# Forgetting attention on one core: where the inverse row sums are turned and spread, and how two key tiles' transposes and products follow each other

## The chip, the cores and the metric

One core of one Trainium2 chip runs one launch of a two-block transformer layer. The metric is device time in microseconds (us) of that launch, lower is better. The matmul engine is TensorE (PE, with its weight loads as PEld), VectorE is DVE, ScalarE is ACT, GpSimd is POOL, and SyncE (SP) issues the DMAs.

## The reference, cut to what matters

The launch runs a first block (retention, sliding-window attention, an MLP), then a second (pooling mixer, forgetting attention, an MLP), all in fp32 on 1024 tokens of width 1024. The change touches only the forgetting attention of the second block: 8 heads of 64, 1024 queries, causal, with a bias from summed log forget gates.

```python
log_f = jax.nn.log_sigmoid(f_logit.astype(jnp.float32)).transpose(0, 2, 1)
cf = jnp.cumsum(log_f, axis=-1)
...
    s = jnp.einsum('bhqd,bhkd->bhqk', qb, k, preferred_element_type=jnp.float32) * scale
    s = s + cq[..., :, None] - cf[..., None, :]
    s = jnp.where(kpos[None, :] <= qpos[:, None], s, NEG_INF)
    p = jax.nn.softmax(s, axis=-1)
    return jnp.einsum('bhqk,bhkd->bhqd', p.astype(v.dtype), v)
```

## The kernel before, in words

Every product is made in fp32r from a high part and a low part of each operand, so most come as two or three matmuls. Large weight products fill the span before and after the attention; the attention runs from about 1695 to 1843 us.

**Units and steps.** The work is cut into 16 units u: 4 pairs of heads t, for each the lower and the upper half of the queries (Q = 0, 1), for each both heads j of the pair. `ITEMS` lists the 8 items idx = (t, Q), so u = 2 idx + j. A unit has four query tiles ii. Its scores have 128 to 512 keys for Q = 0 and 640 to 1024 for Q = 1. `attention_order` (L373) is the one order that all engines follow: at step s and tile ii it does the scores of the next tile, the exponentials of tile (s, ii), and then, for unit s-1, one "turn" (Q = 0) or two (Q = 1). A turn n is one tile of 128 keys.

- `scores` (L1021): TensorE makes query x key products (L1049, L1050) and adds the mask (L1051). VectorE takes the row minimum of the negated scores (L2397). The two score bank pairs alternate, so a tile's scores wait for the exponential of the tile two before it.
- `weights` (L1662): ScalarE takes the exponential into `Pu`, and the row sum into `st` (L1667).
- `turned` (L1056): TensorE transposes up to four 128x128 tiles of `Pu` into one PSUM bank (L1062), ScalarE copies it as the high part `PAh` (L1675), VectorE subtracts to get the low part `PAl` (L2402).
- `values` (L1067) of turn n - `LAG` (2): value x `PAh` and value x `PAl` (L1078, L1079) add up the unit's output in bank 6 or 7.

The transposed tiles take turns in two PSUM banks, 4 and 5 (`ring.turn([4, 5])`, L1007). A turn therefore waits for `PAl` of the turn two before it. The same ring also serves the two small products below, each of which takes one place in it and shifts the banks of the turns behind.

**The end of a unit (`tail`).** After the last `values` of a unit a generator is advanced once per turn. VectorE computes the inverse sums of both heads of an item (`inverse`, L2408: four small instructions, L2415, L2418, L2422, L2423) when the first head's unit ends; ScalarE copies half of the output bank to `ot` (L1687), VectorE adds (L2435). Two advances later TensorE transposes the inverse sums `n4` to rows (bank group `nT`, L1095) for j = 0, and ScalarE copies them to `rw` (L1693); for j = 1 TensorE spreads them over 128 partitions with one product (`rl`, L1103), and VectorE multiplies the output by that bank (L2440). POOL then splits the scaled output into the high and low parts (L2659, L2661) that the output projection reads. POOL also prepares the next pair's operands (`stack`, L2606), and SyncE copies them by DMA (L2983, L2985).

Where each small piece stands before, in the order of a turn:

```python
for _ in range(1 + ITEMS[(s - 1) // 2][1] if s else 0):
    turned(n, *TURNS[n])
    if n >= LAG:
        values(n - LAG, *TURNS[n - LAG])
        ...
    for g in tails:
        next(g, None)
```

## Time and profile before

| what | value |
|---|---|
| median of 3 runs | 2570.13 us (2567.49 to 2576.94) |
| profiled execution | 2573.41 us, its span 2571.6 us |
| mean granted TensorE clock | 0.998 of full |
| DVE, ACT, POOL busy, whole span | 57%, 41%, 7% |
| share of PE in the chain that ended last | 89% |
| attention (first scores to the last spreading product) | about 1695.5 to 1842.6 us |
| first scores of the third pair of heads | 1762.0 us |

The profile counts an engine as busy while an instruction is in flight. TensorE's matmuls overlap: a row of the timeline tells when each started, and the distance between two starts is what one costs in a full pipe. In a timeline row the columns are start, duration, engine, line, operation, output<-inputs, shape and count, and in brackets the idle time before it with what ended it.

### The profile page before, as it was taken

What the parts mean: (1) busy time and instruction counts of PE and PEld (TensorE: products, weight loads), DVE (VectorE), ACT (ScalarE), POOL (GpSimd) and SP (SyncE); (2) the same over time, 40 slices, a digit from 0 to 9 for tenths busy, and PEclk for the clock granted to TensorE, in tenths of its full rate; (3) what the DMA queues carried; (4) which work ended last, traced back from release to release, by engine and by line L of the source; (5) the groups of instructions that cost most, each with busy time, mean ns of one, the idle gap of its engine ahead of it and who ended that gap; (6) DMA issues with size and microseconds to landing.
All of it is one profiled execution on the core that took longest, in us unless ns stands there. A gap on an engine that the chain in (4) does not pass through costs nothing.

```text
span 2571.6 us, 30682 instructions
## 1 busy us (share of the span) xinstructions
PE 2524.5 (98%) x12072; PEld 2084.9 (81%) x12072; DVE 1473.5 (57%) x2153; ACT 1056.3 (41%) x1698; POOL 189.0 (7%) x173
## 2 busy tenths in 40 slices
PE   7999999999999999999999999999999999999998
PEld 6777888888888788888888887877788888888886
DVE  4345223323533777666664754358768676576668
ACT  4344322223212544444434543357526444444432
POOL 0000000000020200000000110154111000000000
PEclk9999999999999999999999999999999999999999
DMA  4221211111422426547865541111313464588554
GB/s 165 67 73 66 74 41 42 34 33 66 147 82 82 143 87 218 184 150 260 306 249 183 185 157 59 34 26 34 115 50 131 140 225 137 175 319 327 183 191 166
DMA packets 129679, 347.59 MB, mean 135 GB/s; under 512 B 13152, under 2 KB 13408, under 8 KB 129408
## 3 DMA queue, kind: packets, MB, share of 16 engines
q1 hardware_dynamic: 129536, 345.63, 38.5%
q8 instruction: 96, 1.57, 0.3%
q14 instruction: 47, 0.39, 0.0%
HBM read 256.91 MB, written 85.52 MB: 133 GB/s over the span
## 4 chain that ended last, share of the span: by engine, by line
PE 89%; DVE 5%; issue 3%; DMA 1%; ACT 1%; POOL 1%; SPq 0%; DVEq 0%; ACTq 0%; POOLq 0%
PE bank L635 27%; PE bank L637 27%; PE bank L636 27%; DVE PAl L2402 1%; DVE st L2397 1%; PE bank L696 1%; POOL accX L2584 1%; PE bank L1062 1%; PE bank L746 1%; PE bank L813 1%; DMA rbx<-wp_d 0%; PE bank L817 0%; PE bank L823 0%; PE bank L781 0%; DVE wlo L1735 0%
## 5 line engine op out<-in xcount | busy, mean ns | idle before, releaser
L1735 DVE TENSOR_TENSOR wlo<-raw,whi 128x1024 fp32r<-128x1024 f32 x102 | 125.2, 1235 | 254.1 <-ACT whi L1138 253.4
L635 PE MATMUL bank<-hhi,whi 128*128 128x512 f32 x608 | 249.6, 411 | 1.7 <-DVE hlo L1760 1.7
L637 PE MATMUL bank<-hhi,wlo 128*128 128x512 f32 x608 | 239.3, 394 | 0.0
L636 PE MATMUL bank<-hlo,whi 128*128 128x512 f32 x608 | 238.6, 392 | 0.0
L1138 ACT ACTIVATE whi<-raw 128x1024 fp32r<-128x1024 f32 x102 | 106.6, 1054 | 103.9 <-PE bank L637 88.2
L635 PEld LDWEIGHTS bank<-hhi,whi 128*128 128x128 f32 x608 | 115.1, 189 | 29.0 <-issue 6.7
L637 PEld LDWEIGHTS bank<-hhi,wlo 128*128 128x128 f32 x608 | 114.9, 189 | 25.2
L636 PEld LDWEIGHTS bank<-hlo,whi 128*128 128x128 f32 x608 | 115.3, 190 | 22.3
L1443 ACT ACTIVATE r<-r 128x512 f32<-128x512 f32 x78 | 49.1, 629 | 137.6 <-DVE r L2220 100.0
L635 PE MATMUL bank<-yhi,whi 128*128 128x512 f32 x192 | 75.0, 391 | 0.0
L637 PE MATMUL bank<-yhi,wlo 128*128 128x512 f32 x192 | 74.8, 390 | 0.0
L636 PE MATMUL bank<-ylo,whi 128*128 128x512 f32 x192 | 74.8, 390 | 0.0
L635 PE MATMUL bank<-whi,hhi 128*128 128x256 f32 x256 | 74.4, 290 | 0.0
L636 PE MATMUL bank<-wlo,hhi 128*128 128x256 f32 x256 | 72.5, 283 | 0.0
L637 PE MATMUL bank<-whi,hlo 128*128 128x256 f32 x256 | 72.5, 283 | 0.0
L635 PE MATMUL bank<-uw0bh,uw0ah 128*128 128x512 f32 x176 | 68.9, 391 | 0.8 <-DVE uw0bl L2172 0.7
L636 PE MATMUL bank<-uw0bl,uw0ah 128*128 128x512 f32 x176 | 68.6, 390 | 0.0
L637 PE MATMUL bank<-uw1bh,uw1al 128*128 128x512 f32 x176 | 68.6, 390 | 0.0
L637 PE MATMUL bank<-uw0bh,uw0al 128*128 128x512 f32 x176 | 68.6, 390 | 0.0
L635 PE MATMUL bank<-uw1bh,uw1ah 128*128 128x512 f32 x176 | 68.6, 390 | 0.0
L636 PE MATMUL bank<-uw1bl,uw1ah 128*128 128x512 f32 x176 | 68.6, 390 | 0.0
L2593 POOL TENSOR_TENSOR accX<-accX,acc 128x1024 f32<-128x1024 f32 x8 | 20.2, 2519 | 609.7 <-DVE acc L2279 609.7
(477 smaller groups left out, 7206.6 us busy)
## 6 DMA issues: line engine op xcount, KB each, us to landing
ra<-ud_d SPq DMA_DIRECT2D x112, 512.0 KB, 4.5
raw<-wp_d SPq DMA_DIRECT2D x102, 512.0 KB, 3.5
rbh<-wp_d SPq DMA_DIRECT2D x64, 512.0 KB, 5.7
rawp<-wp_d SPq DMA_DIRECT2D x26, 1024.0 KB, 5.8
ud_d<-us SPq DMA_DIRECT2D x104, 256.0 KB, 5.4
rbw<-wp_d SPq DMA_DIRECT2D x48, 512.0 KB, 3.6
ud_d<-f SPq DMA_DIRECT2D x76, 256.0 KB, 2.0
rbx<-wp_d SPq DMA_DIRECT2D x32, 512.0 KB, 7.6
```

Of the source, the lines that this page charges most:

```text
L635: e.matmul(P, sh, mh, start=first, stop=False, skip_group_check=more)
L636: e.matmul(P, sh, ml, start=False, stop=False, skip_group_check=more)
L637: return e.matmul(P, sl, mh, start=False, stop=last, skip_group_check=more)
L696: i = e.transpose(P[:, 128 * j:128 * j + 128], src[:, 128 * k:128 * k + 128], ident[:, :])
L746: i = e.matmul(P[:, 256 * (m % 2) + j0:256 * (m % 2) + 256], qs[64 * g:64 * g + 64, m, 128 * n:128 * n + 128], ks[64 * g:64 * g + 64, 128 ...
L813: x = e.matmul(P[:, 0:256], ss[n % 2][:, :], rv[i][:, n, :], start=True, stop=n == 0)
L1062: x = e.transpose(P[:, 128 * ii:128 * ii + 128], Pu[u % 2][ii][:, 128 * k:128 * k + 128], ident[:, :])
L1138: e.activation(whi[n % SLOTS][:, :], raw[n % RAWS][:, :], ACT.Copy).then_inc(*up("whi", n))
L1443: e.activation(r[:, :], r[:, :], ACT.Relu).then_inc(*up("relu", tag, name, p))
L1735: e.tensor_tensor(out=wlo[n % SLOTS][:, :], in0=raw[n % RAWS][:, :], in1=whi[n % SLOTS][:, :].bitcast(F32), op=ALU.subtract).then_inc(*up( ...
L2397: e.tensor_reduce(st[:, m:m + 1], psum[:, b:b + w], AXIS.X, ALU.min).then_inc(*up("mn", u, ii))
L2402: e.tensor_tensor(out=PAl[n % 3][:, c], in0=bank_of("pt", n)[:, c], in1=PAh[n % 3][:, c].bitcast(F32), op=ALU.subtract).then_inc(*free("pt ...
```

## The change

In `attention_order` two callbacks take the place of the later part of the tails. `rows` (transpose of the inverse sums on TensorE, copy to `rw` on ScalarE) is called at tile ii = 2 of every even step from 2, right after the scores and exponentials and ahead of the turns. `spread` (the spreading product, the multiplication on VectorE, the split on POOL) is called at ii = 3 of every odd step from 3, also ahead of the turns, and once at the end. And where a step has two turns per tile, both turns' transposes are issued first, then both turns' products. The number and size of the instructions stay the same.

```diff
@@ -370,7 +370,8 @@
     return max(0, k - 4 * ITEMS[u // 2][1])
 
 
-def attention_order(scores, weights, stack, turned, values, tail, pooled):
+def attention_order(scores, weights, stack, turned, values, tail, rows, spread, pooled):
+
 
     restack, tails = iter(()), []
     scores(0, 0)
@@ -383,23 +384,30 @@
                 scores(*divmod(4 * s + ii + 1, 4))
             if s < 16:
                 weights(s, ii)
+            if ii == 2 and s > 1 and s % 2 == 0:
+                rows(s // 2 - 1)
+            if ii == 3 and s > 2 and s % 2:
+                spread((s - 3) // 2)
             next(restack, None)
             if s == 0:
                 pooled(ii)
-            for _ in range(1 + ITEMS[(s - 1) // 2][1] if s else 0):
+            group = range(n, n + 1 + ITEMS[(s - 1) // 2][1]) if s else ()
+            for n in group:
                 turned(n, *TURNS[n])
+            for n in group:
                 if n >= LAG:
                     values(n - LAG, *TURNS[n - LAG])
                     if TURNS[n - LAG][0] < TURNS[n - LAG + 1][0]:
                         tails.append(tail(TURNS[n - LAG][0]))
                 for g in tails:
                     next(g, None)
-                n += 1
+            n += 1 if s else 0
     for m in range(n - LAG, n):
         values(m, *TURNS[m])
     tails.append(tail(15))
     for g in tails:
         run(g)
+    spread(7)
 def build(nc, I, out, sg, cd, yd, xd, ud):
     with ExitStack() as ctx:
         return programs(nc, ctx, I, out, sg, cd, yd, xd, ud)
@@ -1083,26 +1091,23 @@
             else:
                 x.then_inc(*up("val", n))
 
-        def tail(u):
-            idx, j, t, Q = unit_of(u)
-            yield
-            yield
-            if j == 0:
-                P, free = ring.open("nT", idx)
-                e.wait_ge(*free)
-                e.wait_ge(*ok("n4", idx))
-                for ii in range(4):
-                    x = e.transpose(P[0:34, 128 * ii:128 * ii + 128], n4[:, 34 * ii:34 * ii + 34], ident[:, :])
-                x.then_inc(*ring.full("nT", idx))
-            else:
-                P, free = ring.open("rl", idx)
-                e.wait_ge(*free)
-                e.wait_ge(*ok("free", "nT", idx))
-                if idx == 0:
-                    e.wait_ge(*ok("n40", 2))
-                e.matmul(P[:, :], sel[:, :], rw[:, :], start=True, stop=True).then_inc(*ring.full("rl", idx))
-
-        attention_order(scores, nothing, lambda t: idle(8), turned, values, tail, pooled)
+        def rows(idx):
+            P, free = ring.open("nT", idx)
+            e.wait_ge(*free)
+            e.wait_ge(*ok("n4", idx))
+            for ii in range(4):
+                x = e.transpose(P[0:34, 128 * ii:128 * ii + 128], n4[:, 34 * ii:34 * ii + 34], ident[:, :])
+            x.then_inc(*ring.full("nT", idx))
+
+        def spread(idx):
+            P, free = ring.open("rl", idx)
+            e.wait_ge(*free)
+            e.wait_ge(*ok("free", "nT", idx))
+            if idx == 0:
+                e.wait_ge(*ok("n40", 2))
+            e.matmul(P[:, :], sel[:, :], rw[:, :], start=True, stop=True).then_inc(*ring.full("rl", idx))
+
+        attention_order(scores, nothing, lambda t: idle(8), turned, values, lambda u: idle(2), rows, spread, pooled)
         tally.alias(("att_end",), ring.latest)
         ring.turn(range(8))
 
@@ -1685,14 +1690,14 @@
             if u > 1:
                 e.wait_ge(*ok("free", "ov", u - 2))
             e.activation(ot[own, :], bank_of("ov", u)[o:o + 64, :], ACT.Copy).then_inc(*up("oal", u))
-            yield
-            if j == 0:
-                e.wait_ge(*ok("full", "nT", idx))
-                if idx:
-                    e.wait_ge(*ok("full", "rl", idx - 1))
-                e.activation(rw[:, :], bank_of("nT", idx)[0:34, :], ACT.Copy).then_inc(*free("nT", idx))
-
-        attention_order(nothing, weights, lambda t: idle(8), turned, nothing, tail, pooled)
+
+        def rows(idx):
+            e.wait_ge(*ok("full", "nT", idx))
+            if idx:
+                e.wait_ge(*ok("full", "rl", idx - 1))
+            e.activation(rw[:, :], bank_of("nT", idx)[0:34, :], ACT.Copy).then_inc(*free("nT", idx))
+
+        attention_order(nothing, weights, lambda t: idle(8), turned, nothing, tail, rows, nothing, pooled)
         feed.cap = NPIECES
         e.wait_ge(*ok("clo", 7))
         feed.ahead(CAT + 5)
@@ -2433,13 +2438,14 @@
             if j == 0 and idx > 1:
                 e.wait_ge(*ok("clo", idx - 2))
             e.tensor_tensor(out=o[own, :], in0=bank_of("ov", u)[own, :], in1=ot[own, :], op=ALU.add).then_inc(*free("ov", u))
-            yield
-            if j:
-                e.wait_ge(*ok("free", "ov", u))
-                e.wait_ge(*ok("full", "rl", idx))
-                e.tensor_tensor(out=o[:, :], in0=o[:, :], in1=bank_of("rl", idx)[:, :], op=ALU.mult).then_inc(*free("rl", idx))
-
-        attention_order(scores, nothing, lambda t: idle(8), turned, nothing, tail, pooled)
+
+        def spread(idx):
+            o = ov[idx % 2]
+            e.wait_ge(*ok("free", "ov", 2 * idx + 1))
+            e.wait_ge(*ok("full", "rl", idx))
+            e.tensor_tensor(out=o[:, :], in0=o[:, :], in1=bank_of("rl", idx)[:, :], op=ALU.mult).then_inc(*free("rl", idx))
+
+        attention_order(scores, nothing, lambda t: idle(8), turned, nothing, tail, nothing, spread, pooled)
         feed.cap = NPIECES
         feed.ahead(CAT + 5)
 
@@ -2648,12 +2654,9 @@
         run(stack(0))
         ones_rows()
 
-        def tail(u):
-            idx, j, t, Q = unit_of(u)
-            if j == 0:
-                return
+        def spread(idx):
+            t, Q = ITEMS[idx]
             c = slice(512 * Q, 512 * Q + 512)
-            yield from idle(4)
             e.wait_ge(*ok(*latest))
             e.wait_ge(*ok("free", "rl", idx))
             e.tensor_copy(chi[4 + t][:, c], ov[idx % 2][:, :]).then_inc(*up("cho", idx))
@@ -2662,7 +2665,7 @@
                             op=ALU.subtract).then_inc(*up("clo", idx))
             latest[:] = "clo", idx
 
-        attention_order(nothing, nothing, stack, nothing, nothing, tail, nothing)
+        attention_order(nothing, nothing, stack, nothing, nothing, lambda u: idle(2), nothing, spread, nothing)
         e.wait_ge(*ok("wt_end", 2))
         e.wait_ge(*ok(*latest))
         e.tensor_copy(chi4[:, :], chi[4][:, :].bitcast(F32)).then_inc(*up("chi4", 0))
```

## Rows read from the trace of the kernel before

**Rows 1.** The page, busy time of TensorE over the whole span.
```profile
PE 2524.5 (98%) x12072; PEld 2084.9 (81%) x12072; DVE 1473.5 (57%) x2153; ACT 1056.3 (41%) x1698; POOL 189.0 (7%) x173
```
**Rows 2.** Windows: stretch, length, busy of PE, PEld, DVE, ACT, POOL, granted clock, DMA.
```profile
1702.00:1842.00 140.00, 127.77 (x769) 96.71 (x767) 119.94 (x217) 108.92 (x247) 58.91 (x63) 0.98 0.13 31
1717.00:1753.00 36.00, 32.84 (x202) 25.09 (x202) 32.03 (x57) 29.08 (x67) 22.58 (x24) 0.99 0.17 39
```
**Rows 3.** Waits, 1695 to 1850 us: us in total, times, longest.
```profile
DVE PAl L2402 <- ACT PAh L1675: 14.4, 23, 1.4
...
PE bank L1095 <- DVE PAl L2402: 6.6, 7, 1.3
```
**Rows 4.** Timeline of TensorE, the first transpose of inverse sums, item 0.
```profile
1713.66 0.23 PE L1051 MATMUL bank<-maskb,identb 128*128 128x128 bf16 x1
...
1715.71 0.34 PE L1079 MATMUL bank<-PAl,v 128*128 128x384 f32 x1
1717.05 0.61 PE L1095 MATMUL bank<-ident,n 128*34 128x128 f32 x4 [1.00 <-DVE PAl L2402]
1717.96 0.51 PE L1049 MATMUL bank<-KH,QS 128*128 128x512 f32 x1 [0.29 <-ACT Pu L1667]
```
**Rows 5.** Timeline of VectorE, the same place.
```profile
1714.95 0.58 DVE L2423 TENSOR_TENSOR n<-st,nh 128x8 f32<-128x8 f32 x1
1715.46 1.21 DVE L2397 TENSOR_REDUCE st<-bank 128x1 f32<-128x1024 f32 x1
...
1719.04 0.96 DVE L2397 TENSOR_REDUCE st<-bank 128x1 f32<-128x768 f32 x1 [0.52 <-PE bank L1051]
```
**Rows 6.** Timeline of ScalarE, the same place.
```profile
1714.46 0.37 ACT L1675 ACTIVATE PAh<-bank 128x256 fp32r<-128x256 f32 x1
1714.86 0.59 ACT L1687 ACTIVATE ot<-bank 64x512 f32<-64x512 f32 x1
1716.70 1.11 ACT L1667 ACTIVATE Pu<-bank,st 128x1024 f32<-128x1024 f32 x1 [1.24 <-DVE st L2397]
...
1717.96 0.58 ACT L1693 ACTIVATE rw<-bank 34x512 fp32r<-34x512 f32 x1
```
**Rows 7.** Timeline of TensorE, the other transposes of inverse sums with a long wait.
```profile
1733.23 0.61 PE L1095 MATMUL bank<-ident,n 128*34 128x128 f32 x4 [0.67 <-DVE PAl L2402]
...
1750.90 0.61 PE L1095 MATMUL bank<-ident,n 128*34 128x128 f32 x4 [1.28 <-DVE PAl L2402]
...
1786.60 0.61 PE L1095 MATMUL bank<-ident,n 128*34 128x128 f32 x4 [1.31 <-DVE PAl L2402]
...
1835.58 0.62 PE L1095 MATMUL bank<-ident,n 128*34 128x128 f32 x4 [1.33 <-DVE PAl L2402]
```
**Rows 8.** Timeline of VectorE, the multiplication by the spread sums.
```profile
1724.44 0.68 DVE L2440 TENSOR_TENSOR ov<-ov,bank 128x512 f32<-128x512 f32 x1
```
**Rows 9.** Timeline of TensorE: product pair and next transposes, at two clocks.
```profile
1721.42 0.47 PE L1078 MATMUL bank<-PAh,v 128*128 128x512 f32 x1
...
1721.97 0.60 PE L1062 MATMUL bank<-ident,Pu 128*128 128x128 f32 x4
...
1838.47 0.77 PE L1078 MATMUL bank<-PAh,vrest 128*128 128x512 f32 x1
...
1839.47 0.63 PE L1062 MATMUL bank<-ident,Pu 128*128 128x128 f32 x2
```
**Rows 10.** Timeline of POOL, the last operand of the third pair's preparation.
```profile
1749.43 1.26 POOL L2630 TENSOR_TENSOR QS<-q,QS 64x512 fp32r<-64x512 f32 x1
```
**Rows 11.** Windows around the two drops of the granted clock, and an earlier one.
```profile
1750.00:1754.00 4.00, 2.64 (x11) 1.87 (x12) 4.00 (x7) 2.51 (x5) 0.69 (x1) 0.76 0.17 37
1835.00:1839.00 4.00, 2.85 (x14) 2.19 (x15) 2.40 (x4) 1.34 (x3) 0.00 (x0) 0.80 0.41 135
...
1512.00:1515.00 3.00, 3.00 (x23) 2.74 (x22) 2.90 (x2) 2.21 (x5) 2.05 (x1) 1.00 0.02 5
```
**Rows 12.** Chain of waits, sixteen transposes of another stage in a row.
```profile
1512.34 1.75 PE bank L696 x16
```

## The prediction

> **What bounds the kernel now.** I read the page first: TensorE is in flight 98% of the span [rows 1], so the time moves only where TensorE's stream gets shorter or loses an idle stretch. The windows come next, cut to the one stage that the diff touches. In the attention from 1702 to 1842 us VectorE is busy 119.9 of 140 us, ScalarE 108.9, TensorE in flight 127.8; from 1717 to 1753 VectorE has 32.0 of 36 [rows 2]. No engine is full: three take turns in being late, VectorE most. The reader is to see that this caps the change: all of VectorE's idle time there is 140 - 119.9 = 20.1 us, 0.8% of the kernel, and a reordering can win only part of it. The waits then say what is late: VectorE waits 14.4 us for the copies PAh, and TensorE 6.6 us in seven places ahead of the transposes of the inverse sums, each time for the PAl that frees the bank [rows 3]. Five of the seven are shown: 1.00, 0.67, 1.28, 1.31 and 1.33 us [rows 4, 7]. These waits are what the moved pieces stand in.
>
> **The change, part by part.** It adds and removes no instruction, so each cost is one of position. Items alternate between one turn per tile (Q = 0) and two (Q = 1), and the cases differ.
>
> *1. Transposing the inverse sums, items with Q = 0 (four).* Today it stands behind the turn of ii = 3 and waits for a PAl [rows 4]. Now it stands ahead of the turn of ii = 2, one turn earlier, when VectorE has not finished the inverse: its last instruction ends at 1714.95 + 0.58 = 1715.53 [rows 5]. TensorE would be there after the mask product of 1713.66, which costs under 0.1: it stands 1.8 us, longer than today's 1.00. Behind it is the turn's own transposes, and behind those, on ScalarE, a whole row: the sums' transposes end 0.61 later at 1716.14, the copy to rw takes 0.58 (to 1716.7), the turn's PAh 0.4 (1717.1), the copy to ot 0.59 (1717.7), and only then the exponential of 1024 keys, which started at 1716.70 today [rows 6]. It is 1.0 late. The scores at 1717.96 wait for just that exponential [rows 4], and VectorE's next minimum, at 1719.04, for those scores [rows 5]. So I put +1.0 on three of the four places. The fourth, at 1750.90, is followed by a half-clock stretch [rows 11] in which VectorE waits for other reasons: 0. Sum +3.0. The bounds of one place: -1.0 if the removed wait is all won, +1.8 if TensorE's stand is all lost.
>
> *2. The same, items with Q = 1 (three; the fourth has no scores left behind it and stays as it is, 1.33 us and all [rows 7]).* The inverse comes two tiles earlier here, so it is ready. The transposes move behind one tile's scores, and the bank's PAl is done by then. That removes 6.6 - 1.00 - 1.28 - 1.31 - 1.33 = 1.7 us of waits in three places. Given back: the second turn's transposes need the bank that the copy to rw frees. The small transposes take about 0.44 (their 0.61 overlaps the next), the copy 0.58 behind their end, so that turn starts some 0.4 later than in a full pipe. Taken: -0.5 in each, -1.5 in sum, because VectorE, which sets the pace, saves the idle and pays only part of the 0.4. Bounds per place -0.9 and +0.4.
>
> *3. Spreading the sums.* The product moves from behind a turn to behind a tile's scores. Where one turn follows (three items) its bank is needed a tile later: 0. Where two follow (four items), the second one needs the bank that VectorE's multiplication frees. The multiplication (0.68 us [rows 8]) stands behind a minimum and now ahead of the two PAl. Its cover is that the first turn's PAh takes 0.6 anyway; about 0.3 of it shows. Sum +1.2; bounds 0 and 0.7 each. For POOL the split now stands ahead of steps of the operand preparation and waits for that multiplication. The cover: the third pair's preparation ends at 1750.7 [rows 10], 11 us ahead of its first use at 1762.0; cost 0, and even if it stood 2 us longer it would be 0. SP's copies of those operands move with it, under the same cover.
>
> *4. Two turns' transposes in a row.* Today a product pair of 0.55 us (1721.42 to 1721.97 [rows 9]) lies between the two turns' transposes. Without it the second turn is ready 0.55 earlier, of which ScalarE, busy 0.6 with the first copy, can use some 0.3. Against it: the first pair of products now stands behind the second turn's wait. In the Q = 1 scores (four steps) VectorE has no idle time to fill. What remains is one tile in each of three steps where two turns meet small scores: -0.9. Bounds: 0, and 24 tiles x 0.27 = -6.5.
>
> Sum: 3.0 - 1.5 + 1.2 - 0.9 = **+1.8 us**. The profiled execution took 2573.4, so it would take 2575.2; it stood 3.3 above the median, within the runs' own spread. On the median that is 2570.1 + 1.8 = **2571.9**. A measurement of this kernel can tell about 0.5%, 12.9 us, from no change.
>
> **Rivals.**
>
> *The waits are really won (faster).* If VectorE catches up from item 1's lateness in its 20 us of idle time, part 1 is 0 or below: its four removed waits (1.00, 1.28, 1.31 and a small one) become a gain of about 3, with parts 2 and 4 about -5.5. For it: this wait is TensorE's longest in the stage [rows 3]. Against it: ScalarE's order is fixed, and it holds the exponential back [rows 6]. Time: 2564.6.
>
> *The clock falls more often (slower).* Granted clock fell to 1.2 GHz, half, twice in the attention: the windows from 1750 and from 1835 show 0.76 and 0.80, and ahead of each TensorE had stood 1.3 us for the inverse sums [rows 7, 11]. After the equally long stand at 1786.60 and the 1.00 at 1717.05 it did not. At half clock a product pair to the next transposes takes 1839.47 - 1838.47 = 1.00 instead of 0.55 [rows 9], and three such pairs cost 1.4 us. With stands of 1.8 in place of 1.3 it might fall in all four places of part 1: three more drops, +4.2, on top of the 1.8: 2576.1. It decides from the point where a stand is followed by a drop in more than one of the four.
> *The clock falls under rows of transposes (slower).* Part 4 puts up to eight transposes side by side. If that by itself brought a drop in each of the eight units with two turns, at 1.4 us each, the time would be 2571.9 + 11.2 = 2583.1. Against it: sixteen transposes in a row, 1.75 us long, ran with the granted clock at 1.00 [rows 11, 12]. I give it 3%. The Trainium skill ("TensorE: Matmul & The Clock Gate", Part 4: PE-mode transpose) speaks for it: a transpose "doesn't count as PE-busy the same way". The trace does not agree as far as those sixteen go; by the page the 2583.1 would be the likelier time, by the trace the 2571.9.
>
> *The change does nothing.* If the order of the small pieces is absorbed wholly by VectorE's load, all four parts are 0: 2570.1. Also, the sums' product would then not stand "behind" a finished inverse at all where Q = 0, which is what part 1 says.
>
> **How the numbers follow.** Forecast (+0.5 to +4 us) 45%; waits won 27%; nothing 12%; clock by stands 10%; clock by transposes 3%; something else 3%. The likeliest gives 2571.9. For the range I take in the won waits (2564.6) and the clock rival (2576.1), and the runs' spread of some 2 us around a median of three, cut where 2 in 10 are left out: 2564.5 to 2577.5. Only a case that goes past 12.9 us leaves the middle: the gain would have to be two thirds of VectorE's idle time, 2%; the loss would need all upper bounds at once (4 x 1.8 + 3 x 0.4 + 4 x 0.7 = 11.2) with clock drops, or the drops under transposes, 4%.
>
> **What would show each step right or wrong.** Part 1: in the timeline of the changed kernel the first sums' transposes start at the end of L2423 and not of a PAl, with about 1.8 us idle before, and the exponential behind them begins about 1 us later relative to its minimum. Part 2: near 1733 they start with no wait, and the second turn's transposes wait for ScalarE's rw. Part 3: the transposes behind a spreading product wait for L2440. Part 4: VectorE's wait for PAh (14.4 us) shrinks by under 2 us. Clock: the windows tell how many stretches are at half clock. The length from the first scores to the last spreading product, 147 us now, should be about 149. I am wrong if it is under 145 or over 153.

## The result, and the profile after

The changed kernel takes 2581.76 us (median of 7 runs, 2578.14 to 2582.34) where the kernel before, beside it, takes 2570.13 (7 runs, 2567.06 to 2576.94): a ratio of 1.0043, 95% interval 1.0034 to 1.0052. It is slower by 0.43%. That lies inside the 0.5% that I had called no change, but 4.3 us above the upper end of my range, and my forecast of +1.8 us was wrong: it is +11.6. The profiled execution took 2582.21 us, its span is 2580.4.

All of it is in the attention. Measured from the start of the first scores to the start of the last spreading product, the attention took 146.6 us before (1695.51 to 1842.12) and 157.85 after (1693.80 to 1851.65), +11.25. By the sign given beforehand ("wrong if under 145 or over 153") the working is wrong, not only its size.

The page and the windows of the changed kernel (stretch, length, busy of PE, PEld, DVE, ACT, POOL, granted clock, DMA), which answer to [rows 1, 2, 11]. Its lines are those of before plus 4 to 8: transposes L1070, products L1086 and L1087, scores L1057 to L1059, copy PAh L1680, PAl L2407, sums' transposes L1099, spreading product L1108.

```profile
PE 2524.2 (98%) x12072; PEld 2084.5 (81%) x12072; DVE 1475.4 (57%) x2153; ACT 1057.0 (41%) x1698; POOL 189.8 (7%) x173
```
```profile
1701.00:1851.00 150.00, 127.86 (x764) 98.50 (x763) 120.97 (x216) 109.25 (x246) 59.44 (x62) 0.98 0.12 29
...
1750.00:1754.00 4.00, 2.45 (x16) 1.95 (x16) 2.94 (x4) 3.11 (x5) 3.71 (x5) 1.00 0.30 70
1801.00:1805.00 4.00, 3.56 (x16) 3.25 (x16) 1.58 (x4) 1.37 (x5) 1.89 (x2) 0.61 0.00 0
1839.00:1843.00 4.00, 4.00 (x20) 3.73 (x18) 1.23 (x4) 1.72 (x4) 1.56 (x2) 0.57 0.00 0
```

The busy times are the same as before, over 150 us instead of 140: each engine does the same work and waits longer. There are two stretches at half clock, as before, in other places, so the clock does not fall more often; what the two cost is worked out under *Two parts at a time*. The mean granted clock of the 7 runs is 0.9966, that of 31 runs of before 0.9965. The waits are (who waits <- whose work ended it: us in total, times, longest), 1693 to 1853 us, against [rows 3]:

```profile
DVE PAl L2407 <- ACT PAh L1680: 21.3, 41, 1.4
ACT PAh L1680 <- PE bank L1087: 15.3, 22, 1.2
ACT PAh L1680 <- PE bank L1070: 10.2, 20, 1.4
...
PE bank L1057 <- ACT Pu L1672: 5.4, 6, 1.9
PE bank L1099 <- DVE n L2428: 5.4, 4, 1.7
PE bank L1108 <- DVE PAl L2407: 3.4, 4, 1.0
```

Four things are to be seen. VectorE's wait for PAh grew from 14.4 to 21.3 us, where I had it shrink. TensorE's wait ahead of the sums' transposes did not go away, it changed its cause: 5.4 us for the inverse (L2428), plus 1.1 in one place for a PAl, where 6.6 stood. The spreading product (L1108) waits for a PAl in four places, 3.4 us, where the kernel before has four waits of 0.1. And the second row is of a kind that the kernel before does not have at all: ScalarE's copy PAh is held back 22 times, 15.3 us in all, by a *product* (L1087). I had named neither of these two.

The three signs of parts 1 to 3 are all there. Timeline of TensorE of the changed kernel, first item, then at 1725 and at 1733 us (start, duration, line, output<-inputs, shape, and in brackets the idle time with what ended it), against [rows 4, 7]:

```profile
1711.98 0.23 PE L1059 MATMUL bank<-maskb,identb 128*128 128x128 bf16 x1
1713.93 0.60 PE L1099 MATMUL bank<-ident,n 128*34 128x128 f32 x4 [1.72 <-DVE n L2428]
...
1717.33 0.50 PE L1057 MATMUL bank<-KH,QS 128*128 128x512 f32 x1 [0.94 <-ACT Pu L1672]
...
1727.60 0.33 PE L1070 MATMUL bank<-ident,Pu 128*128 128x128 f32 x1 [0.45 <-DVE ov L2446]
...
1733.62 0.61 PE L1099 MATMUL bank<-ident,n 128*34 128x128 f32 x4
1734.25 0.66 PE L1070 MATMUL bank<-ident,Pu 128*128 128x128 f32 x4
1735.32 0.55 PE L1070 MATMUL bank<-ident,Pu 128*128 128x128 f32 x3 [0.41 <-ACT rw L1698]
```

The stand of 1.72 us until the inverse is done (I said 1.8; in the other three places of part 1 it is 1.48, 1.47 and 0.72); at 1727.60 the wait for VectorE's multiplication behind a spreading product; at 1733.62 no wait, and then 0.41 for the copy to rw (I said 0.4). VectorE and ScalarE at the first item, against [rows 5, 6]:

```profile
1713.71 1.21 DVE L2402 TENSOR_REDUCE st<-bank 128x1 f32<-128x1024 f32 x1
```
```profile
1714.57 0.59 ACT L1698 ACTIVATE rw<-bank 34x512 fp32r<-34x512 f32 x1 [1.71 <-PE bank L1099]
1715.06 0.36 ACT L1680 ACTIVATE PAh<-bank 128x256 fp32r<-128x256 f32 x1
1715.45 0.59 ACT L1692 ACTIVATE ot<-bank 64x512 f32<-64x512 f32 x1
1716.07 1.11 ACT L1672 ACTIVATE Pu<-bank,st 128x1024 f32<-128x1024 f32 x1
```

The minimum ended at 1713.71 + 1.21 = 1714.92, the exponential started at 1716.07: 1.15 us later, where before it was 0.03. That is part 1 as predicted, at this place. What was left to explain was therefore mainly part 4.

### The profile page after: what moved, and what is told of

Same layout as the page of the kernel before. It is cut to its first block, busy times and chain, and to the rows that moved or that the text cites. A ratio compares the mean times of both kernels' runs of the same rounds, so it can differ in the third digit from the quotient of the medians.

```text
span 2580.4 us, 30682 instructions
## 1 busy us (share of the span) xinstructions
PE 2524.2 (98%) x12072; PEld 2084.5 (81%) x12072; DVE 1475.4 (57%) x2153; ACT 1057.0 (41%) x1698; POOL 189.8 (7%) x173
## 4 chain that ended last, share of the span: by engine, by line
PE 90%; DVE 4%; issue 2%; ACT 2%; DMA 1%; POOL 1%; SPq 0%; DVEq 0%; ACTq 0%; POOLq 0%
PE bank L643 28%; PE bank L645 28%; PE bank L644 28%; PE bank L1070 1%; DVE PAl L2407 1%; PE bank L704 1%; POOL accX L2590 1%; PE bank L754 1%; PE bank L821 1%; DVE st L2402 1%; ACT PAh L1680 0%; PE bank L831 0%; PE bank L825 0%; PE bank L789 0%; DVE wlo L1740 0%
## 5 line engine op out<-in xcount | busy, mean ns | idle before, releaser
L2407 DVE TENSOR_TENSOR PAl<-bank,PAh 128x512 fp32r<-128x512 f32 (+1 forms) x96 | 52.6, 555 | 22.5 <-ACT PAh L1680 21.3
```

Of the source, the lines that this page charges most:

```text
L2407: e.tensor_tensor(out=PAl[n % 3][:, c], in0=bank_of("pt", n)[:, c], in1=PAh[n % 3][:, c].bitcast(F32), op=ALU.subtract).then_inc(*free("pt ...
```

## The experiments

All kernels but the fourth-buffer ones differ from before or after in order and in banks alone; every one computes the whole layer. "Step s" is the stretch from the first scores of unit s to those of unit s+1 (step 15: to the last spreading product), from the timeline of TensorE. The parts became switches:

```diff
+            if ii == 2 and s > 1 and s % 2 == 0 and s // 2 - 1 in ROWS_MOVED:
+                rows(s // 2 - 1)
+            if ii == 3 and s > 2 and s % 2 and (s - 3) // 2 in SPREAD_MOVED:
+                spread((s - 3) // 2)
...
+            group = list(range(n, n + 1 + ITEMS[(s - 1) // 2][1])) if s else []
+            for part in ([group] if PAIRED else [[m] for m in group]):
+                for n in part:
+                    turned(n, *TURNS[n])
+                for n in part:
+                    if n >= LAG:
+                        values(n - LAG, *TURNS[n - LAG])
```

An item that is not moved has its piece in the tail, as before. All results, the kernel before being run beside each group (medians 2569.7 to 2570.8). The ratio is that of the record and not the quotient of two medians (for e1 the medians give 1.0013). The attention is that of one profiled execution each:

| run | pairs | rows moved | spread moved | banks, buffers | median us | ratio, 95% | attention us | half-clock stretches |
|---|---|---|---|---|---|---|---|---|
| before | | | | | 2570.1 | | 146.60 | 2 |
| after | x | x | x | | 2581.76 | 1.0043, 1.0034 to 1.0052 | 157.85 | 2 |
| e1 | x | | | | 2574.02 | 1.0004, 0.9994 to 1.0013 | 150.03 | 0 |
| e2 | | x | | | 2574.41 | 1.0013, 1.0003 to 1.0022 | 150.44 | 1 |
| e3 | | | x | | 2569.13 | 0.9994, 0.9984 to 1.0004 | 144.94 | 0 |
| e4 | | x | x | | 2574.51 | 1.0012, 1.0002 to 1.0021 | 151.06 | 1 |
| e5 | x | x | x | own banks | 2574.64 | 1.0014, 1.0005 to 1.0024 | 150.97 | 1 |
| e6 | | | x | own banks | 2565.24 | 0.9976, 0.9967 to 0.9985 | 141.99 | 1 |
| e7 | | Q = 1 items | | | 2570.86 | 1.0005, 0.9995 to 1.0014 | 144.51 | 0 |
| e8 | | x, one tile later | x | own banks | 2564.60 | 0.9976, 0.9966 to 0.9985 | 140.10 | 0 |
| e9 | x | x, one tile later | x | own banks | 2569.25 | 0.9990, 0.9980 to 1.0000 | 144.69 | 0 |
| e10 | x | | x | | 2576.36 | 1.0025, 1.0015 to 1.0034 | 151.93 | 2 |
| e11 | x | x | | | 2580.59 | 1.0040, 1.0026 to 1.0054 | 155.43 | 2 |
| e12 | | x, one tile later | two-turn places and the end | own banks | 2563.71 | 0.9973, 0.9964 to 0.9983 | 140.09 | 0 |
| e13 | x | | | nT own, third bank | 2569.74 | 0.9996, 0.9987 to 1.0005 | 144.92 | 0 |
| e14 | | | | nT own, third bank | 2565.63 | 0.9984, 0.9975 to 0.9993 | 139.91 | 0 |
| e15 | | as e12 | as e12 | e12 + third bank | 2563.40 | 0.9971, 0.9960 to 0.9981 | 139.03 | 0 |
| e16 | x | | | nT own | 2572.49 | 1.0007, 0.9997 to 1.0016 | 149.31 | 1 |
| e17 | x | | | 4th PAh, PAl | 2572.31 | 1.0003, 0.9994 to 1.0013 | 147.34 | 0 |
| e18 | x | | | e13 + 4th PAh, PAl | 2567.24 | 0.9983, 0.9974 to 0.9992 | 143.59 | 1 |

Where a half-clock stretch falls varies, so steps are compared where neither kernel has one.

**The parts alone, and all but the pairs.**

```diff
+ROWS_MOVED = ()            # range(8) in e2, e4
+SPREAD_MOVED = ()          # range(8) in e3, e4
+PAIRED = True              # e1; False in e2, e3, e4
```

> Two turns' transposes first, then two turns' products; the two small products where they were before. Time against before, and length of the attention (146.6 us before, 157.9 after the whole change). Ring theory (a small product ahead of a pair of turns takes one of only two PSUM banks): no small product is moved, so -1 to +1 us, attention about 147. Inverse theory (the transposes of the inverse sums wait for an unfinished inverse): 0 as well. Pairs theory (products now stand behind the second turn's wait): +5 us or more, attention above 151.

> Only the transposes of the inverse sums are moved, in all eight items. Inverse theory: TensorE's stands of 1.0 to 1.9 us in four places cost all they last, +7 us or more, attention above 153. Ring theory: +1 to +4 us, since the stands are partly won back by the wait that is gone, and only the items with two turns pay for the bank. Pairs theory: 0.

> Only the spreading product (with its multiplication and split) is moved. Ring theory: about +1 to +1.8 us in each of the four places ahead of a pair of turns, so +4 to +7 us, attention 151 to 154. Inverse theory and pairs theory: 0, attention 146 to 148.

> The whole change but for the pairs: both small products moved, turns one by one as before. Ring theory: most of the 11 us stays, +7 to +10. Inverse theory: all of it stays, +10 to +12. Pairs theory: most of it goes, +4 or less.

These texts set three theories against each other. The ring theory failed in e3 (attention 144.94, where it had 151 to 154), the inverse theory in e4 (151.06, 4.5 us above before, where it had 10 to 12); the pairs theory came near in e1 (150.03, where it had above 151) and in e4 (it had +4 or less), and e2 (+3.8) lies in the range of the ring theory.

No single part makes the 11 us. The ratios of e1, e2 and e3 add up to 1.0011, the whole is 1.0043; e4 without pairs is 1.0012, so the pairs cost 0.3% on top of the rest. Steps without a half-clock stretch say where (us):

| step | before | e1 pairs | e2 rows | e3 spread | e4 rows, spread | after |
|---|---|---|---|---|---|---|
| 2 + 3 | 17.92 | 18.47 | 18.98 | 17.08 | 18.21 | 18.31 |
| 4 | 9.79 | 10.73 | 9.81 | 11.01 | 11.03 | 11.55 |
| 5 | 5.02 | 5.42 | 5.02 | 5.03 | 5.03 | 5.42 |
| 6 | 7.08 | 7.08 | 9.45 | 7.39 | 9.28 | 9.29 |

Rows moved: +1.06 in steps 2 + 3. Pairs: +0.55 there, then +0.94 and +0.40, in each of the steps 3 to 5 where I had put nothing or a gain. The waits of e1, 1694 to 1846 us:

```profile
DVE PAl L2426 <- ACT PAh L1699: 14.6, 29, 1.1
ACT PAh L1699 <- PE bank L1106: 11.8, 23, 0.9
```

L1106 is the product on PAl. So the new wait comes with the pairs alone.

**A kernel before without its drops.** e7 moves the rows of items 1, 3, 5, 7 only:

```diff
+ROWS_MOVED = (1, 3, 5, 7)
```

> The transposes of the inverse sums are moved only in the items with two turns per tile, where the inverse is long done. Inverse theory: moving them in all items cost 3.8 us of attention, all of it in the items with one turn, so here -1 to +0.5 us against before. Ring theory: +1 to +2 us, since the second turn waits for the copy that frees the bank.

Its steps are those of before within 0.04 us, but for the two in which before has a half-clock stretch (step 7: 13.77 against 12.89; step 15: 24.69 against 23.46). So this part of the change is worth nothing, and e7's trace, all at full clock, is the base for what follows: 144.51 us. The two stretches cost before 0.9 + 1.2 us.

**Order or bank?** A transpose group, `nT` and `rl` all take places in the ring of two PSUM banks. e5 is the whole change with the spreading products of even items in bank 1 and the sums' transposes of odd items in bank 3, both of the score banks that are free there; e6 does it with the spread moved only; e8 calls `rows` of the Q = 0 items one tile later (ii = 3); e9 is e8 with pairs; e12 is e8 with the spread moved only where two turns follow (items 0, 2, 4 and 6), and at the end.

The waits of the scores that make these banks free in time are not shown.

```diff
-            P, free = ring.open("nT", idx)
+            own_bank = 3 if idx % 2 else None
+            P, free = ring.open("nT", idx, bank=own_bank)
...
-            P, free = ring.open("rl", idx)
+            own_bank = 1 if idx % 2 == 0 else None
+            P, free = ring.open("rl", idx, bank=own_bank)
```
```diff
-            if ii == 2 and s > 1 and s % 2 == 0 and s // 2 - 1 in ROWS_MOVED:
+            if ii == (3 if s % 4 == 2 else 2) and s > 1 and s % 2 == 0 and s // 2 - 1 in ROWS_MOVED:
...
-PAIRED = False
+PAIRED = True
...
-SPREAD_MOVED = range(8)
+SPREAD_MOVED = (0, 2, 4, 6, 7)
```

> The whole change, but the spreading product of four items and the transposes of the inverse sums of the four items with two turns each use a PSUM bank that the scores leave free (1 and 3), so that they take no place between the two banks of the turns. Ring theory (the place in the ring is what a moved small product costs ahead of a pair of turns): the steps with two turns and small scores fall from 11.6 us to 10 or less, three to four of them, so the attention falls from 157.9 to 149 to 153. Pairs theory (a product now stands behind the second turn's wait, whoever holds the bank): it falls by 3 us at most, since pairs alone cost 3.4 us with no small product moved. Inverse theory: no change, 156 to 158.

> Only the spreading product is moved, turns one by one, and the same two own banks. Ring theory: the steps with two turns and small scores fall from 11.0 us (spreading product moved, in the ring) to about 9.0, so the attention is 138 to 141 us and the time 4 to 7 us below before. Theory that those steps are bound by VectorE or by latency in any case: 143 to 145, as with the ring.

> Both small products moved, turns one by one, own banks, and where an item has one turn per tile the transposes of the inverse sums come one tile later (behind the scores of tile 3 instead of 2), when the inverse is finished. Inverse theory: the step before (8.3 us with the transposes at tile 2, 6.2 before) returns to 6.2 to 6.8 and the step behind does not get longer than 11, so the attention is at least 3 us shorter than with the own banks alone, and 138 to 142. If the stand for the inverse is only moved, not removed, it stays at 145 or more.

> The version with both small products moved, own banks and the later transposes of the inverse sums (attention 140.1 us), now with two turns' transposes first and then two turns' products. Only the pairs differ. Pairs theory (a product that was ready waits behind the second turn's bank): +3 to +5 us of attention, 143 to 145.5. Theory that pairs cost only together with a small product in the ring: 139.5 to 141.

> The 140.1 us version, but the spreading product moved only where two turns follow and a bank of its own is free. The step of one turn per tile with large scores was 7.4 us with it moved there and 7.1 before, three of them: so 139 to 139.6 us. If the multiplication has to stand somewhere on VectorE in any case, it stays at 140.1 or goes up.

The banks matter much: e5 takes the whole change from 1.0043 to 1.0014, with step 4 down from 11.55 to 10.33. With own banks the kernel with the spread moved is faster than before (e6, 0.9976, clear of 1; an own bank for the spreading product without the move was not tried). Its attention, 141.99, is just above the 138 to 141 of the ring theory; e5, e8 and e9 lie where the theories named for them had put them. Calling the rows one tile later removes the cost of part 1: steps 2 and 3 of e8 are 6.18 and 10.93 us, in e3, with the rows in the tail, 6.16 and 10.92. It gains nothing either: e8 has the ratio of e6, 0.9976. With pairs, e9 is at 144.69 us, 4.6 above e8. So the pairs cost about as much on a good version as on before. e12 against e8 is nothing: 0.9973 against 0.9976, 140.09 against 140.10 us, where 139 to 139.6 was forecast.

**Two parts at a time.**

```diff
+ROWS_MOVED = ()            # e10; range(8) in e11
+SPREAD_MOVED = range(8)    # e10; () in e11
+PAIRED = True
```

> Pairs and the moved spreading product in the ring, transposes of the inverse sums where they were. The parts alone gave attentions of 150.0 (pairs) and 144.9 (spread), against 144.5 with neither and with the clock never halved. If the parts only add up: 150 to 151. If pairs and a small product in the ring make each other worse: 153 or more, with the step of two turns and small scores at 12 us or more, against 10.7 with pairs alone and 11.0 with the spread alone.

> Pairs and the moved transposes of the inverse sums in the ring, spreading product where it was. The parts alone: 150.0 (pairs) and about 148.5 (transposes, less one halved stretch), 144.5 with neither. If they add up: 153 to 155. If most of what is missing in the whole change (157.9) is between these two: 156 or more. If it is between pairs and spread: 150 to 153.

Neither fits one of its forecasts: e10 (151.93) lies between adding up and making each other worse, e11 (155.43) a little above adding up. By the ratios the pairs go badly with both (e10 1.0025 against 0.9998 for the two alone, e11 1.0040 against 1.0017). By the lengths against the full-clock base of 144.51 there is little left of that: pairs +5.5, rows +5.9 with a half-clock stretch in it, spread +0.4, in sum 11.8 with one stretch; the whole is +13.3 with two. The steps tell more. Adding the parts up step by step (e7 and what e1, e2 and e3 each differ from it), the whole is 2.0 us *below* the sum over the thirteen steps in which none of the five traces has a half-clock stretch. It is above the sum by more than 0.1 us only where it has a stretch itself: step 12 takes 13.14 against 10.14, step 15 25.62 against 24.10. So at full clock the parts do not make each other worse, and by this estimate the two stretches cost the changed kernel some 4.5 us, where the two of before cost 2.1: about 2 of the 11 us are clock. What makes a stretch dearer in one place than in another no run shows.

**Which resource do the pairs run out of?** Two were left: the bank (two turns' transposes in a row need both, so the next pair waits for both PAl), and the buffers PAh, PAl, of which there are three. e13 gives the turns of units 3, 7, 11 and 15 a third PSUM bank and keeps `nT` of odd items out of the ring, with pairs; e14 is the same without pairs; e16 has pairs and `nT` out, no third bank; e15 is e12 with the third bank.

```diff
-            P, free = ring.open("pt", n)
+            third = ITEMS[u // 2][1] and u % 2
+            if k == 0:
+                cycle[:] = [ring.order[ring.at], ring.order[1 - ring.at], 1]
+            P, free = ring.open("pt", n, bank=cycle[k % 3] if third else None)
```

> Pairs alone, with the transposes of the inverse sums of two-turn items in a bank of their own, and in the four units where the scores beside the turns leave bank 1 free the turns go round three banks instead of two. Bank theory of the pairs (the second turn waits for a bank, and ready products stand behind it): in these units the wait between the two turns' transposes goes, and the step of two turns and small scores falls from 10.7 us to 9.3 or less, with the step behind it from 5.4 to 5.0. Theory that rows of transposes cost by themselves: it stays within 0.3 us of the kernel with pairs and two banks.

> The same banks, turns one by one and all small products where they were. If the two banks bind there too: step of two turns and small scores 9.8 us before, 9.0 or less here, last stretch 23.5 before, 22.5 or less. If VectorE or the latency of transposes, copy and subtraction bind: within 0.3 us of 9.8 less the 0.8 us of the removed wait.

> Pairs alone with the transposes of the inverse sums of two-turn items in a bank of their own, two banks for the turns. It tells the third bank from the own bank. Bank theory: the step of two turns and small scores keeps 9.9 to 10.3 us of the 10.7, as the waits between the two turns' transposes are still there. If the small product in the ring was all that pairs cost: 9.3 or less.

> The best version so far (spreading product moved in five items, transposes of the inverse sums later, own banks; attention 140.1 us) with the third bank for the turns. Bank theory: 137 to 139 us. Theory that VectorE binds it by now (126 us busy of 142): 139.5 to 140.5.

Both bank edits together are worth 4.6 us without pairs (e14, 139.91 against 144.51), the third bank by itself about 3 with them (e13 against e16, 149.31 less some 1.5 for e16's half-clock stretch in step 7, 14.95 against 13.46). The pairs go on costing 5.0 us (e13 against e14). So the bank is a limit of this kernel, but not what the pairs suffer from. The waits of ScalarE in e13, then in e14 (the product on PAl is L1115, the transposes L1098):

```profile
ACT PAh L1711 <- PE bank L1115: 9.0, 22, 0.8
ACT PAh L1711 <- PE bank L1098: 4.4, 13, 0.8
```
```profile
ACT PAh L1711 <- PE bank L1098: 10.5, 26, 0.9
```

The wait for the product is there with three banks, and only with pairs. Of the forecasts, e13 missed (step 4 at 9.74 us, where the bank theory had 9.3 or less), e14 (step 4 at 8.64, step 15 at 22.02) and e16 (step 4 at 9.96) came as the bank theory had them, and e15 at 139.03 is at the upper edge of its 137 to 139. ScalarE's copy of turn n writes the buffer of turn n-3 and waits for that turn's product (`val n-3`). e17 adds a fourth PAh and PAl to e1, in memory that is free only from the turns of unit 9 on; e18 does the same to e13.

```diff
+    PAh.append(at("PAh3", FO + 32, [128, 512], F32R))
+    PAl.append(at("PAl3", FO + 34, [128, 512], F32R))
...
-            if n >= 3:
-                e.wait_ge(*ok("val", n - 3))
+            if n == FOURTH:
+                e.wait_ge(*ok("val", 47))
+            elif n >= 3:
+                e.wait_ge(*ok("val", n - (4 if n > FOURTH else 3)))
```

> Pairs alone, but from unit 9 on (step 10 and later, where the values of the second pair of heads are dead and give the room) PAh and PAl have four buffers instead of three, so that ScalarE's copy of turn n waits for the product of turn n-4 and not n-3. Buffer theory of the pairs: in these steps the copy of the second turn no longer waits for a product that stands behind that turn's own transposes; pairs cost 2.2 us there over turns one by one (steps 9 to 15), and at least 1.3 of it goes: last stretch 24.3 to 23.6 or less, step 11 12.55 to 12.1 or less. Bank theory, or TensorE's order alone: nothing changes by more than 0.3 us, though the wait's row gets shorter.

> Pairs with three banks in the steps that have a bank free (144.9 us of attention) and the four buffers from unit 9 on. If buffers and banks are all that pairs cost: steps 12 and 15 fall to those of the three banks with turns one by one, 8.4 and 22.0 (22.7 with pairs). If a part lies in TensorE's order itself, step 15 stays above 22.5.

Because the buffer comes halfway, each of these kernels holds its own control. Windows (columns as above), steps 3 to 8 and steps 11 to 15, of e7 (no pairs, three buffers), e1 (pairs, three) and e17 (pairs, four in the second stretch only):

```profile
1712.21:1768.59 56.38, 50.48 (x316) 38.95 (x317) 49.62 (x90) 44.47 (x100) 34.86 (x39) 1.00 0.17 39
1780.67:1837.61 56.94, 50.74 (x316) 38.38 (x315) 47.75 (x89) 43.59 (x96) 7.97 (x9) 1.00 0.08 24
```
```profile
1713.34:1773.06 59.72, 51.70 (x315) 38.78 (x316) 52.36 (x90) 44.37 (x100) 35.86 (x39) 1.00 0.16 37
1785.54:1844.24 58.70, 52.78 (x315) 38.54 (x314) 48.34 (x89) 43.86 (x96) 7.98 (x9) 1.00 0.08 23
```
```profile
1712.28:1772.04 59.76, 51.71 (x315) 38.79 (x316) 52.38 (x90) 44.38 (x100) 35.88 (x39) 1.00 0.16 37
1784.53:1840.51 55.98, 51.73 (x315) 38.46 (x315) 47.27 (x89) 43.07 (x96) 8.00 (x9) 1.00 0.08 24
```

In the first stretch the pairs cost 3.3 us, with or without the edit (59.72 and 59.76 against 56.38). In the second they cost 1.8 with three buffers (58.70 against 56.94) and nothing with four: 55.98 is 1.0 *below* the unpaired kernel. The wait goes with it; from 1780 us on ScalarE's waits for PAh in e1, then in e17 (product L1106 and L1116, transposes L1089 and L1099):

```profile
ACT PAh L1699 <- PE bank L1106: 6.0, 11, 0.9
...
ACT PAh L1699 <- PE bank L1089: 2.9, 9, 0.8
```
```profile
ACT PAh L1711 <- PE bank L1099: 7.0, 14, 1.0
```

e18 agrees (step 15: 21.28 us, 22.74 in e13, 22.02 in e14), and is faster than before, 0.9983. The forecasts of the buffer theory held in both (e17: step 15 at 22.40, step 11 at 12.04; e18: step 12 at 8.43). The whole runs follow: the fastest of e17 is 2.5 us below the fastest of e1 (2570.19, 2572.68), that of e18 3.6 below that of e13 (2564.45, 2568.02), though the ratios of e17 and e1 (1.0003, 1.0004) do not tell them apart. The fourth buffer was tried with pairs only, so how much of the last 1.0 us belongs to the pairs and how much to the buffer is open, as is the first half, where there was no room for one.

One place shows the mechanism. ScalarE of e1, and TensorE of e1, where unit 11's turns go in pairs:

```profile
1803.01 0.60 ACT L1699 ACTIVATE PAh<-bank 128x512 fp32r<-128x512 f32 x1 [0.28 <-PE bank L1089]
1804.27 0.60 ACT L1699 ACTIVATE PAh<-bank 128x512 fp32r<-128x512 f32 x1 [0.66 <-PE bank L1106]
```
```profile
1802.32 1.39 PE L1089 MATMUL bank<-ident,Pu 128*128 128x128 f32 x8
1803.47 0.47 PE L1105 MATMUL bank<-PAh,vrest 128*128 128x512 f32 x1
1803.78 0.39 PE L1106 MATMUL bank<-PAl,vrest 128*128 128x512 f32 x1
```

Both turns' transposes end at 1802.32 + 1.39 = 1803.71, and ScalarE has been free since 1803.61. But the second copy starts at 1804.27, 0.1 after the end of the *first* product pair behind those transposes (1803.78 + 0.39 = 1804.17). That is 0.56 us lost, about the 0.55 of a product pair, and e1 has 23 such waits.

## Why the prediction was wrong

Against e7 the parts measured, with what I had in brackets: part 1 +5.9 (+3.0), part 2, which is e7 against before, 0 (-1.5), part 3 +0.4 (+1.2), part 4 +5.5 (-0.9).

**Part 4 is the step that failed, in its sign.** I wrote that "without it the second turn is ready 0.55 earlier, of which ScalarE ... can use some 0.3", sum -0.9, and bounded the cost by 0. Measured, it is +5.5 us alone (e1 against e7), +4.6 (e9, e8), +5.0 (e13, e14), in traces with no half-clock stretch in the attention. The fastest whole runs of the same three couples differ by 5.3, 4.0 and 4.9 us, their medians by 3.2, 4.7 and 4.1; the ratios of e1 and e7 alone (1.0004, 1.0005) show no difference, and why is open. The trace of e7 is a good execution of it: granted clock 0.999, where its ten runs have 0.9967 in the mean. I looked at when the second turn's transposes are done, and not at what else its copy needs. In the order of before, products n-2 stand ahead of the transposes of turn n+1, so the copy of turn n+1, which overwrites the buffer of turn n-2, finds it free. In pairs the products n-2 stand behind those transposes, which first wait for a bank. The second turn of each pair can gain nothing from being transposed early, and loses whatever its transposes waited, and at the place shown above, where the timeline has no wait ahead of them, the length of the products themselves. I even wrote that "the first pair of products now stands behind the second turn's wait", and did not ask who waits for that product. VectorE and ScalarE sit in the chain bank, PAh, PAl, bank, so the delay is paid.

**Part 1 was right in three places and wrong in the fourth.** e2 against e7 gives +1.06, +1.09 and +1.11 (steps 2 + 3, 10 + 11, 14 + 15), by the stand and the late exponential as worked out, where I had +1.0. The fourth place I let be 0 because a half-clock stretch follows it in before, and it cost 2.7 us in e2 (steps 6 + 7: 22.64 against 19.97), which has a stretch of its own there. That is not all clock. Between the changed kernel and e10, which differ by the moved rows alone and have both no stretch there, the place costs 1.55 (20.65 against 19.10), where steps 2 + 3 and 10 + 11 cost 1.09 and 1.10. Between the copy to rw and the exponential ScalarE has one copy more there, of a piece of weights, and TensorE stands twice as long for the exponential as at 1717.33:

```profile
1751.60 1.05 ACT L1143 ACTIVATE whi<-raw 128x1024 fp32r<-128x1024 f32 x1
```
```profile
1754.55 0.50 PE L1057 MATMUL bank<-KH,QS 128*128 128x512 f32 x1 [1.89 <-ACT Pu L1672]
```

**Part 2 was mis-sized**: 0 instead of -1.5 (e7). The wait was not won, it moved on. TensorE's waits for PAl in before, then in e7 (the sums' transposes are L1095 and L1118, the turns' L1062 and L1089):

```profile
PE bank L1095 <- DVE PAl L2402: 6.6, 7, 1.3
...
PE bank L1062 <- DVE PAl L2402: 1.9, 5, 0.6
```
```profile
PE bank L1118 <- DVE PAl L2426: 4.9, 4, 1.3
PE bank L1089 <- DVE PAl L2426: 4.3, 9, 0.7
```

The 1.7 us are gone ahead of the sums' transposes, and 2.4 us more stand ahead of the turns' transposes. The wait for the copy to rw, which I had set against the gain, is not in e7 at all; the changed kernel, with pairs, has it three times, 1.2 us in sum.

**Part 3 was near in sum, by luck, and wrong in place.** e3 against e7 is +0.4 against my +1.2. The first two-turn place costs +0.4 over steps 3 and 4 (21.93 against 21.56), as two amounts that I did not see: 0.8 won, 1.2 lost. The other three win 0.15, 0.5 and 0.25 (steps 7 + 8, 11 + 12, 15), so that the four places for which I had +1.2 won 0.55 together. Each of the three one-turn places costs 0.3 (step 6: 7.39 against 7.08), where I had 0. I asked who waits behind the spreading product, and not what it waits for itself: in the ring it waits for a PAl, four times 0.1 us in before, 1.6 us in sum in e3, 3.4 in the changed kernel, and in none of these places with own banks (e5, e6). I priced each place by itself and not the ring of banks, whose order the move shifts for all turns behind: e5 and e6 show that the banks are worth more than the whole term.

**The rivals.** *Waits won* did not happen (its 2564.6 also leaves out part 3's +1.2, with which it would be 2565.9): 6.6 us of waiting at the sums' transposes became 6.5. Even e8, where `rows` comes after the inverse is ready, gains nothing over e6, which leaves it in the tail. *Nothing changes* fell in every part but the second. *Clock by stands*: the stands for the inverse were there (1.72, 1.48, 1.47 and 0.72 us), none of them was followed by a half-clock stretch, and the profile has two stretches as before; the rival's three more did not come. In e11, though, two of its stands, of 1.78 and 1.79 us, were followed by one at once. *Clock under rows of transposes* fell: e1, e9 and e13 issue every two-turn tile's transposes side by side, eight in the row above, and show no half-clock stretch in the attention, while before, without pairs, shows two. The Trainium skill ("TensorE: Matmul & The Clock Gate", Part 4: PE-mode transpose) says that a transpose does not count as PE-busy the same way; these traces do not bear out a price for it here.

**The range** rested on a bound of 0 for part 4's cost. A product pair of 0.55 us in the way of each of 24 tiles would have been +13.2, and that end would have held what came. All upper bounds at once were 11.2 us, and even that is under the measured 11.6. In my chances what came had only the 3% of "something else".

**A version that beats both kernels.** e15, without pairs, with rows one tile later, the spread moved only where two turns follow and at the end, own banks and a third bank: 2563.40 us, 0.9971 (0.9960 to 0.9981) of before and 18 us under the changed kernel. Which of its parts carries it: own banks with the moved spread and late rows give 0.9976 (e8), the third bank with one own bank and nothing moved gives 0.9984 (e14), and together they are hardly more than the first.

## What to carry to other kernels

When two stages of a pipeline are regrouped, list for every instruction all that it waits for, the buffer it overwrites too: with k buffers and a lag of k-1, issuing two producers in a row puts the release of a buffer behind the producer that needs it. It needs one buffer more, or the old order; here the buffer was shown to take the cost away in the second half of the attention only. A small product that shares a ring of two banks with the main stream should get a bank of its own before its place in the order is tuned, and moving work ahead pays only to the point where its input is ready: one tile later cost nothing here, one tile earlier cost 1.1 us in three places and more in the fourth.

## What the runs showed of the hardware

The granted clock goes with much of the spread of the kernel before. Each run lists its mean granted clock, and of the 31 runs of before beside e1 to e4 those at 0.999 took 2567.1 us (5 runs) and those at 0.994 took 2574.6 (4 runs). The half-clock stretches in the attention come at different places in different executions and cost 0.9 and 1.2 us in the trace of before (against e7), 1.5 in e16, and by the estimate above 3.0 and 1.5 in the changed kernel. I had expected them to follow TensorE's long stands. The 20 traces have 14 half-clock stretches in the attention, and each began within 2.4 us after the end of a stand of TensorE of 0.7 to 1.9 us: e11's, from 1752 and 1790 us, right behind stands of 1.78 and 1.79, e10's, from 1797 and 1831, behind stands of 0.78 and 1.04. But the same traces have 127 stands of 0.7 us and more, and behind 113 of them none began within that time; e9, e13, e14 and e15 have no stretch at all there, with stands of up to 1.3 us. So a stand stood ahead of every fall, and its length does not decide; what does, no run here shows.
